# Layer norms summed tile by tile as deviations from a shift, with waits per chunk and eight stores, in a two-block model on one core

## The reference

```python
x = layer_norm(x, ln_in_g, ln_in_b)
for l in range(2):
    ...                       # three attentions from x @ w_in[l], three gates
    merged = sum(gates[:, :, n] * (branch_n @ w_branch[l, n]) for n in range(3))
    mix = merged @ w_out[l]
    x = layer_norm(2 ** 0.5 * x + mix, ln1_g[l], ln1_b[l])
    gu = x @ w_ffn_in[l]      # 1024 -> 2 x 2816
    ffn = (silu(gu[..., :2816]) * gu[..., 2816:]) @ w_ffn_out[l]
    x = layer_norm(2 ** 0.5 * x + ffn, ln2_g[l], ln2_b[l])
```

## Time and profile before

| What | us |
|---|---|
| Median of three runs (3594.59 to 3598.16) | 3596.62 |
| The profiled execution | 3600.81 |
| Its span | 3599.0 |
| PE busy in the span | 3139.0 |
| DVE, ACT, POOL busy | 1547.0, 961.6, 967.6 |

### The profile page before, as it was taken

One profiled execution on the slowest core, in us unless ns is written; L12 is line 12 of the kernel. 1 busy time (PEld: TensorE's weight loads), 2 busy tenths in 40 slices (PEclk: granted clock), 3 DMA queues, 4 the chain that ended last, 5 costly groups with the idle time before them and its releaser, 6 DMA issues.

```text
span 3599.0 us, 33188 instructions
## 1 busy us (share of the span) xinstructions
PE 3139.0 (87%) x13220; PEld 2155.6 (60%) x13220; DVE 1547.0 (43%) x2542; ACT 961.6 (27%) x1354; POOL 967.6 (27%) x353
## 2 busy tenths in 40 slices
PE   4788899878777769999899799996999999879996
PEld 3667565642222247675755578885776665568885
DVE  8895566431110131726356632223444555642223
ACT  3432223220000023425233122212333424222211
POOL 2362211310000024442211334443433212224441
PEclk9989799889999969999899899998999999989998
DMA  5214321269999942121120222221212121112220
GB/s 234 70 53 160 132 95 42 82 257 423 422 422 421 422 185 89 49 92 47 59 71 24 70 82 94 95 105 65 70 53 77 47 82 41 51 61 95 104 94 35
DMA packets 70078, 465.31 MB, mean 129 GB/s; under 512 B 8656, under 2 KB 8944, under 8 KB 17712
## 3 DMA queue, kind: packets, MB, share of 16 engines
q1 hardware_dynamic: 59184, 436.31, 31.5%
q0 software_dynamic: 5056, 16.55, 1.3%
q10 hardware_dynamic: 5696, 10.49, 0.8%
HBM read 450.71 MB, written 12.60 MB: 129 GB/s over the span
## 4 chain that ended last, share of the span: by engine, by line
PE 67%; DMA 13%; DVE 13%; ACT 2%; issue 2%; POOL 1%; SPq 0%; ACTq 0%; DVEq 0%; POOLq 0%
PE ps L424 13%; PE ps L425 13%; PE ps L426 13%; DMA mring<-w 11%; PE ps L662 3%; PE ps L645 2%; PE ps L646 2%; PE ps L647 2%; PE ps L413 2%; PE ps L2108 2%; PE ps L825 1%; DMA wring<-wfirst 1%; PE ps L677 1%; PE ps L928 1%; POOL w_lo L500 1%
## 5 line engine op out<-in xcount | busy, mean ns | idle before, releaser
L500 POOL TENSOR_TENSOR w_lo<-wring,w_hi 128x2048 fp32r<-128x2048 f32 (+1 forms) x200 | 822.6, 4120 | 1890.8 <-ACT w_hi L490 1890.7
L424 PE MATMUL ps<-x_hi,w_hi 128*128 128x512 f32 (+1 forms) x1512 | 615.2, 407 | 53.7 <-POOL w_lo L500 31.4
L426 PE MATMUL ps<-x_hi,w_lo 128*128 128x512 f32 (+1 forms) x1512 | 602.4, 398 | 0.0
L490 ACT ACTIVATE w_hi<-wring 128x2048 fp32r<-128x2048 f32 x176 | 335.6, 1910 | 515.7 <-PE ps L424 404.8
L425 PE MATMUL ps<-xf_lo,w_hi 128*128 128x512 f32 x1112 | 442.1, 398 | 0.0
L424 PEld LDWEIGHTS ps<-x_hi,w_hi 128*128 128x128 f32 (+1 forms) x1512 | 292.7, 194 | 133.3 <-issue 42.5
L426 PEld LDWEIGHTS ps<-x_hi,w_lo 128*128 128x128 f32 (+1 forms) x1512 | 292.5, 193 | 63.6
L2182 PE MATMUL ps<-mring,xT__94 128*64 128x512 f32 x512 | 245.2, 610 | 66.2 <-DMA mring<-w 60.8
L2183 PE MATMUL ps<-mring,xT__94 128*64 128x512 f32 x512 | 245.4, 610 | 0.0
L425 PEld LDWEIGHTS ps<-xf_lo,w_hi 128*128 128x128 f32 x1112 | 214.6, 193 | 43.3
L1961 DVE TENSOR_TENSOR hid<-ps,sil 64x512 f32<-64x512 f32 x32 | 21.8, 682 | 437.7 <-ACT sil L1581 437.7
(11 more groups left out here) (451 smaller groups left out, 5414.1 us busy)
## 6 DMA issues: line engine op xcount, KB each, us to landing
mring<-w SPq DMA_DIRECT2D x192, 1024.0 KB, 28.5
wring<-wlayers SPq DMA_DIRECT2D x148, 1024.0 KB, 4.7
wring<-wfirst SPq DMA_DIRECT2D x60, 1024.0 KB, 4.9
wmodS<-wmod SPq DMA_DIRECT2D x4, 2048.0 KB, 18.3
y_rows<-ysb ACTq DMA_DIRECT2D x64, 128.0 KB, 6.4
rp<-rpb POOLq DMA_DIRECT2D x16, 192.0 KB, 2.7
hT<-xT SPq DMA_DIRECT2D x1, 2048.0 KB, 18.2
xS<-xT SPq DMA_DIRECT2D x1, 2048.0 KB, 7.7
```

The source lines that it names most:

```text
L424: said(pe.matmul(bank, wh[:, 0:m], hi[:, k, :], start=(k == 0), stop=False))
L426: ins = pe.matmul(bank, wl[:, 0:m], hi[:, k, :], start=False, stop=(k == nk - 1))
L490: act.activation(w_hi[:, q % HI_SLOTS, :], wring[:, g % SLOTS, :], ACT.Copy).then_inc(hi_rdy, 1)
L500: ins = pool.tensor_tensor(w_lo[:, slot % SLOTS, o:o + n], wring[:, slot % SLOTS, o:o + n], w_hi[:, q % HI_SLOTS, o:o + n].bitcast(F32), A ...
```

## The change

**The norm** is rewritten (`norm_in_step`, with parts for PE and ACT). DVE first makes x from its two parts for all chunks (8 additions). Tiles 0 to 2 are added as they come. After tile 1 the sum of chunks 0 and 1 goes to PE (`shift_pe`, after tile 2), which gives a shift for each token, their mean. It is subtracted from chunks 0 to 2 and, before the product is there, from `DN_ALPHA * x` of chunks 3 to 7. From then on each tile takes one addition to become a deviation, one to join the sum of deviations, and one that adds the square of the tile before, made by ACT. After the last tile PE sums the deviations and the squares over partitions; the variance is the mean square less the squared mean, a small correction of the shift. The remaining mean is spread by a full-width product (bank 6), the inverse root as before (bank 7), and DVE does three instructions for each chunk: center, scale, low part.

**Other parts.**
- `weights_hi` calls stand between the squares in an order written out by `norm_in_step_act`, one for each slot start.
- In the merge ACT makes `m_hi` and DVE makes the low part of the tile before. `weights_hi` of `out2` stands after the fourth `m_hi`.
- `out2` waits for `merged_rdy` chunk by chunk in its first tile, and the first block's `out` likewise for `mix2_rdy`.
- The first two tiles of `ffn_in` (one A, one B) are made together, chunk by chunk, from weights in that order; `values` makes its first two tiles together.
- In the last norm ACT adds the bias, and SP stores each chunk by itself.
- Semaphores that nothing used are removed.

```diff
+        def norm_in_step_act(act, where, c0, nk):
+            events = [(c, 0, c) for c in range(-(c0 % CHUNKS), nk * DC, CHUNKS)]
+            events += [(nk * (max(c, 2) + 1) + (2 if c > 2 else 1), 1, c) for c in range(DC)]
+            i = cnt["ln_a"]
+            for _, kind, c in sorted(events):
+                if kind == 0:
+                    weights_hi(act, c0 + max(c, 0))
+                else:
+                    act.wait_ge(dev_rdy, DC * i + c + 1)
+                    if DC * i + c >= 2:
+                        act.wait_ge(dev_sq_in, DC * i + c - 1)
+                    act.activation(x_lo_f[where][:, 3 + c % 2, :], hT[:, c, :], ACT.Square).then_inc(dev_sq, 1)
...
+        def shift_pe(pe, where):
+            pe.wait_ge(norm_sums, 2 * cnt["ln_p"] + 1)
+            pe.matmul(ps[:, 4, :], ones, x_lo_f[where][:, 0, :], start=True, stop=True).then_inc(norm_products, 1)
+
+        def norm_in_step_pe(pe, where):
...
+            pe.wait_ge(norm_sums, 2 * i)
+            for r in range(NQB):
+                ins = pe.matmul(ps[:, 4, r:r + 1], dev[:, r * P:(r + 1) * P], ones[:, 0:1], start=True, stop=True)
+            ins.then_inc(norm_products, 1)
+            pe.wait_ge(dev_sq_in, DC * i)
+            for r in range(NQB):
+                ins = pe.matmul(ps[:, 5, r:r + 1], sq[:, r * P:(r + 1) * P], ones[:, 0:1], start=True, stop=True)
+            ins.then_inc(norm_products, 1)
+            pe.matmul(ps[:, 6, :], ones, dev, start=True, stop=True).then_inc(norm_products, 1)
+            cnt["nv_p"] += 1
+            pe.wait_ge(inv_rdy, cnt["nv_p"])
+            for r in range(NQB):
+                ins = pe.matmul(ps[:, 7, r * P:(r + 1) * P], n_inv[:, r:r + 1].broadcast_to((P, P)), ident, start=True, stop=True)
+            ins.then_inc(norm_products, 1)
...
+        def norm_in_step(dve, where, to, g, b):
...
             for c in range(DC):
+                n = mark(TT(hT[:, c, :], x_hi[:, c, :].bitcast(F32), X[:, c, :].bitcast(F32), ALU.add))
+            dve.wait_ge(dve_step, n)
+            for m in range(3):
+                STT(out=hT[:, m, :], in0=hT[:, m, :], scalar=DN_ALPHA, in1=B.take(dve), op0=ALU.mult, op1=ALU.add).then_inc(B.free, 1)
+                dve.wait_ge(B.free, B.took)
+                if m == 1:
+                    TT(shift, hT[:, 0, :], hT[:, 1, :], ALU.add).then_inc(norm_sums, 1)
+            dve.wait_ge(norm_products, 5 * i + 1)
+            step(TS(shift, ps[:, 4, :], 1.0 / (2 * P), None, ALU.mult))
+            for c in range(3):
+                TT(hT[:, c, :], hT[:, c, :], shift, ALU.subtract).then_inc(dev_rdy, 1)
+            for c in range(3, DC):
+                n = mark(STT(out=hT[:, c, :], in0=hT[:, c, :], scalar=DN_ALPHA, in1=shift, op0=ALU.mult, op1=ALU.subtract))
+            dve.wait_ge(dev_rdy, DC * i + 3)
+            step(TT(dev, hT[:, 0, :], hT[:, 1, :], ALU.add))
+            step(TT(dev, dev, hT[:, 2, :], ALU.add))
+            dve.wait_ge(dve_step, n)
+            square_in(0)
+            square_in(1)
+            for m in range(3, DC):
+                square_in(m - 1)
+                TT(hT[:, m, :], B.take(dve), hT[:, m, :], ALU.add).then_inc(dev_rdy, 1)
+                free_bank_b(dve)
+                dve.wait_ge(dev_rdy, DC * i + m + 1)
+                ins = TT(dev, dev, hT[:, m, :], ALU.add)
+                if m < DC - 1:
+                    step(ins)
+            ins.then_inc(norm_sums, 1)
+            square_in(DC - 1)
...
+            for c in range(DC):
+                if c + 1 < DC:
+                    ready.append(center(c + 1))
+                dve.wait_ge(dve_step, ready[c])
+                y = hT[:, c, :] if to is None else x_lo_f[to][:, c, :]
+                STT(out=y, in0=hT[:, c, :], scalar=g[:, c:c + 1], in1=ps[:, 7, :], op0=ALU.mult, op1=ALU.mult).then_inc(t_rdy, 1)
+                if to is not None and c >= 1:
+                    low(c - 1)
...
             def values(c0, wait=None):
-                for j in range(NQB):
-                    b = A.claim(pe)
+                for group in ((0, 1), (2,), (3,)):
+                    b = {j: A.claim(pe) for j in group}
...
-            pe.wait_ge(merged_rdy, (l + 1) * 3 * DC)
             for m in range(DC):
-                tile3(pe, B.claim(pe), base["out2"] + m * DC, m_hi, m_lo, DC).then_inc(B.full, 1)
-            mean_pe(pe)
-            norm_pe(pe, DC)
-            for m in range(FFC):
-                tile3(pe, A.claim(pe), base["ffn_in"] + 2 * m * DC, *xf, DC,
-                     wait=(lambda k: pe.wait_ge(x_rdy, 2 * DC * l + DC + k + 1)) if m == 0 else None).then_inc(A.full, 1)
+                tile3(pe, B.claim(pe), base["out2"] + m * DC, m_hi, m_lo, DC,
+                      wait=(lambda k: pe.wait_ge(merged_rdy, (3 * l + 2) * DC + k + 1)) if m == 0 else None).then_inc(B.full, 1)
+                if m == 2:
+                    shift_pe(pe, 0)
+            norm_in_step_pe(pe, 0)
+            first = A.claim(pe), B.claim(pe)
+            for k in range(DC):
+                pe.wait_ge(x_rdy, 2 * DC * l + DC + k + 1)
+                for n, b in enumerate(first):
+                    wh, wl = chunk(pe, base["ffn_in"] + 2 * k + n)
...
             for m in range(DC):
-                weights_hi(act, end1 + l * size2 + two["out2"] + m * DC)
-            squares(act, hT, DC, lambda c: act.wait_ge(centered, DC + 2 * DC * l + c + 1))
-            root(act)
+                act.wait_ge(branches_in, l * DC + m + 1)
+                act.activation(m_hi[:, m, :], uT[:, m, :], ACT.Copy, scale=0.5).then_inc(m_hi_rdy, 1)
+                if m == DC // 2 - 1:
+                    weights_hi(act, base["out2"])
+            norm_in_step_act(act, 0, base["out2"], DC)
             norm_hi(act, (V(f"ln1_b{l}"), 1))
...
+                    if m == 0:
+                        dve.wait_ge(merged_rdy, k)
+                    TT(uT[:, m, :], uT[:, m, :], g, ALU.add).then_inc(branches_in, 1)
+                    if m >= 1:
+                        merged_low(m - 1)
...
-            sp.wait_ge(x_rdy, DC + 2 * DC * LAYERS)
-            sp.dma_start(out, hT[:]).then_inc(stored, 16)
-            sp.wait_ge(stored, 16)
+            for c in range(DC):
+                sp.wait_ge(out_rdy, c + 1)
+                sp.dma_start(out[:, c, :], hT[:, c, :]).then_inc(stored, 16)
+            sp.wait_ge(stored, 16 * DC)
...
-            pe.wait_ge(mix2_rdy, DC)
             for m in range(DC):
-                tile3(pe, B.claim(pe), one["out"] + m * DC, mix_hi, mix_lo, DC).then_inc(B.full, 1)
+                tile3(pe, B.claim(pe), one["out"] + m * DC, mix_hi, mix_lo, DC,
+                      wait=(lambda k: pe.wait_ge(mix2_rdy, k + 1)) if m == 0 else None).then_inc(B.full, 1)
```

More of the change, by code:

```diff
@@ L566, in add_up @@
             dve.wait_ge(summed, cnt["sum"])
[L568 to L576, removed]
+        def shift_pe(pe, where):
+            pe.wait_ge(norm_sums, 2 * cnt["ln_p"] + 1)
+            pe.matmul(ps[:, 4, :], ones, x_lo_f[where][:, 0, :], start=True, stop=True).then_inc(norm_products, 1)
+        def norm_in_step_pe(pe, where):
+            cnt["ln_p"] += 1
+            i = cnt["ln_p"]
+            dev, sq = x_lo_f[where][:, 1, :], x_lo_f[where][:, 2, :]
+            pe.wait_ge(norm_sums, 2 * i)
[12 more added lines that the diff above has]
+            ins.then_inc(norm_products, 1)
         def mean_pe(pe):
@@ L1002, in layer_pe @@
                 tile3(pe, B.claim(pe), base["ffn_out"] + m * FFC, g_hi, g_lo, FFC,
-                     wait=(lambda k: pe.wait_ge(hid_rdy, l * FFC + k + 1)) if m == 0 else None).then_inc(B.full, 1)
-            mean_pe(pe)
-            norm_pe(pe, DC)
+                      wait=(lambda k: pe.wait_ge(hid_rdy, l * FFC + k + 1)) if m == 0 else None).then_inc(B.full, 1)
+                if m == 2:
+                    shift_pe(pe, 1)
+            norm_in_step_pe(pe, 1)
         def layer_act(act, l):
@@ L1250, in layer_dve @@
                 merge(2, m)
-            def residual(where):
-                for m in range(DC):
-                    STT(out=hT[:, m, :], in0=x_hi[:, m, :].bitcast(F32), scalar=DN_ALPHA, in1=B.take(dve), op0=ALU.mult, op1=ALU.add).then_inc(B.free, 1)
-                    dve.wait_ge(B.free, B.took)
-                    step(STT(out=hT[:, m, :], in0=x_lo[where][:, m, :].bitcast(F32), scalar=DN_ALPHA, in1=hT[:, m, :], op0=ALU.mult, op1=ALU.add))
-                    if m >= 1:
-                        add_up(dve, hT, m)
-            residual(0)
-            center(dve, hT)
-            normed_split(dve, hT, 1, V(f"ln1_g{l}"), V(f"ln1_b{l}"))
+            merged_low(DC - 1)
+            norm_in_step(dve, 0, 1, V(f"ln1_g{l}"), V(f"ln1_b{l}"))
             for m in range(FFC):
@@ L1269, in layer_dve @@
             assert a == A2 + (l + 1) * A_LAYER, (a, A2, A_LAYER)
[L1270 to L1275 removed]
+            norm_in_step(dve, 1, 0 if l < LAYERS - 1 else None, V(f"ln2_g{l}"), V(f"ln2_b{l}"))
```

(3 more changed lines are left out.)

126 lines of the change are left out of this document (80 added, 46 removed).

## The result

The changed kernel took 3538.14 us (median of four runs, 3535.15 to 3542.07) against 3595.61 us for the kernel before beside it: a ratio of 0.984, 95% interval 0.9823 to 0.9857. The forecast was 3546 with a range of 3527 to 3562; the measured time lies at the lower edge of the range of the forecast case alone, 3538 to 3556. Timed once more, on another chip, it took 3537.65 (five runs) against 3598.84, ratio 0.9834 (0.9817 to 0.9851). The profiled execution has a span of 3540.24 us, 58.8 less than before.

The account below looks back on a forecast made before the run. The prediction took TensorE, busy 87% of the span, as the bound, with gains only where it waits. Gains of 10.4 + 19.9 + 13.9 + 1.3 + 5.5 = 51.0 us gave 3546 us, range 3527 to 3562.

Parts of the forecast that it names:

- forecast case: Whole kernel: the main case, with the stall in out2 and no w_lo in the tails, 3538 to 3556 us, chance 0.54.
- LN1 and `out2`, 5.2 each: Second block's out2 and first norm: shorter tail less a stall at tile 5, 5.2 us gained per layer, 10.4 for two.
- The merge, counted as 0: Merge before out2: held low parts and a low clock at tile 4 cancel the gain; bounds 5 gained, 4 lost.
- LN2 of layer 0, 19.9: Second norm of layer 0 up to the first values tiles: tail 26.4 us in place of 47.9, 19.9 gained after deductions.
- The end, 13.9: Last norm and store: span ends 22.8 us after the last tile's first DVE instruction, before 37.6; 13.9 us gained.
- z: In each norm, the start of the first DVE instruction on the last projection tile; tail times count from it.
- The first block, 5.5: First block's out, waiting for mix2_rdy by chunk: 2.70 us idle and 2.8 us of low clock go, 5.5 gained.
- `values` of layer 0, 1.3: First two values tiles of layer 0, made together: 1.3 us gained, between 0 and 2.
- A (no stall): Rival in out2: DVE's run gets ahead of GpSimd or tile 5's bank is free in time; 3533 us, chance 0.2.
- B: Rival: a w_lo falls into the 23-instruction tail of the three inner norms, 5.1 us each; 3561 us, chance 0.17.
- C: Rival: slower by DVE alone, if the tails' 84 instructions cost over 1.27 us each; 3616 us at 1.5, chance 0.03.
- D: Rival: PE stays behind the new waits, its pair starting only when all chunks stand; 3582 us, chance 0.06.

Follow-up runs that it names:

- first moved wait: Changed kernel, but in out2's norm ACT makes the w_hi of tile 3's start only after the square of tile 3: 3529.19 us, ratio 0.9806.
- moved waits: Changed kernel, but in out2's norm ACT makes tile 3's w_hi after that tile's square and the last w_hi after the norm's eight high parts: 3515.26 us.
- moved waits and pieces together: Changed kernel with both w_hi of out2's norm made later and GpSimd's w_lo beside merge and out2 in four instructions: 3508.53 us, ratio 0.9746.
- the pieces: Changed kernel, but GpSimd makes the w_lo beside the merge and out2's first tiles in four instructions of 128x512, not one: 3519.98 us, ratio 0.9783.

## Why the prediction came out as it did

The forecast case happened: the stall in `out2` came where it was put, no `w_lo` fell into the tails, and the time was in the range. It was 8 us too slow, since three of its terms were too careful: the merge, LN2 and the end, each in part about the granted clock. That the column sums ran at full clock in both LN2 and the end was partly luck.

- **LN1 and `out2`, 5.2 each: 4.7 in layer 0 and 6.0 in layer 1 measured** (the three stretches from `out2` to the end of `ffn_out`), 10.7 for 10.4. These stretches also hold the product behind tile 2 of `ffn_out`, 0.95 in the forecast, which it took off LN2 and the end. Step by step it held: low parts of m = 0 and m = 4 held (4.64 and 4.65 us), 3.3 us idle before tile 5 (3.33), the low clock behind it, `out2` 7.0 longer (6.6, 5.5), tile 7 read 1.9 late (2.0), the pair finished 27.8 behind PE's last tile (27.9).
- **The merge, counted as 0, was the mis-sized step.** The prediction took 2.8 us for a low clock after the idle before tile 4. In layer 0 there was none (clock 1.00), and 3.7 us were gained; in layer 1 it came (0.50 at 3078), and still 2.1 were gained from the last branch's first tile to `out2` (30.4 for 32.5). The whole stretch of layer 1 doesn't show it (628.1 against 626.7), since stretches of 600 us carry clock differences of several microseconds from one execution to the next. The bounds, 5 gained to 4 lost, held both. The two stretches together gained 2.7.
- **LN2 of layer 0, 19.9: 22.5 measured**, or 21.6 with the 0.95 of the product taken off. The column sums ran at full clock, 1.05 and 1.03 in place of two times 1.87, for 1.7 us. The prediction had taken the low-clock row, though PE's idle before them was 11.89 there and is 2.05 now. But full clock was not certain: behind the same idle of 2.05 us the two groups took 1.95 to 1.99 us in seven of the twelve profiles and 2.25 to 3.35 in five. With the first moved wait, an edit that doesn't touch this norm, they ran mostly at the low clock and LN2 took 38.1 us. The hold by `w_lo` was as forecast (1.16 for 0.69). The wait for the A bank was smaller than the 0.7: PE's next matmul started 0.40 us behind the pair's last one, where 0.23 is usual.

```profile
2418.72 1.65 PE L602 MATMUL ps<-cs,uT 128*128 128x1 f32 x8 [2.05 <-DVE uT L668]
...
2420.22 1.85 PE L606 MATMUL ps<-cs,uT 128*128 128x1 f32 x8
```

- **The end, 13.9: 17.6 measured**, z + 20.1 for z + 22.8; the other 0.95 is the product, which falls before z. Column sums at full clock again 1.7 (behind an idle of 1.58; in five of the twelve profiles they took 2.15 to 3.16 us in place of 1.95); DVE's chunks 1.26 apart for 1.32, 0.5 in all; the store 2.0 us for 3.0, or 2.46 from ACT's end at 3537.78 to the end of the span, 0.5 in all. The two rows that bounded it, 192 KB in 2.7 and 1024 KB in 4.7, gave no lower end: a store of 256 KB was faster than both. The estimate from the Trainium skill's page "DMA: Bandwidth & Descriptors", section "Anatomy of one DMA — SWDGE (gpsimd) path", 2.6 for the last store by a fit for DMAs that GpSimd issues (these are SyncE's), is nearer than the 3.0, and is also above what was measured. The last store is issued at about z + 18, not z + 20.
- **The first block, 5.5: 5.6. `values` of layer 0, 1.3:** the second tile's copy followed the first matmul by 13.2 us in place of 15.2, but of these 2.0 us only 0.4 are left at the last value copy.

Of the rivals, A (no stall) didn't happen, and the moved waits show what it would have been worth: its 12 us for two layers are 10 to 15 in the stretches of `out2`, by the execution they are set against. Its cause, a DVE run that keeps GpSimd out, is excluded by the row of five in 7.50 us beside a `w_lo` of 4.86: about 0.3 lost by GpSimd, some 4 by DVE. The Trainium skill, page "SBUF — State Buffer", section "Who interferes with whom", has the issue order decide who blocks; the trace agrees in the sense that GpSimd enters between two DVE instructions and then holds the next for its whole length. The run with moved waits and pieces together shows that this costs the changed kernel 27 us by the stretches and 29 by the medians. B fell by the absence of any held instruction between the spread and the last low part; C by a pace of 0.64 us an instruction; D by PE's first pair matmul at 14 us behind the last tile, not behind all chunks.

## What to carry to other kernels

When sums over a tensor are moved into the production of its tiles, the instructions that used to follow now compete with everything that runs beside the tiles; look for the engine whose instructions hold the summing one's (here GpSimd's `w_lo`, 4.6 us each), move its work by where it is requested, or cut it into pieces, before counting the gain. A tail that waits on a chunked producer gains when two consumers share each chunk (14 us here), and to a wait of PE belongs the low clock that may follow it, which can be bounded but not counted on.

## What the runs showed of the hardware that was not expected

- Idle PE of 2.66 us was followed by no fall of the granted clock (1983.25), by one that came 1.5 us later and lasted some 3 (1997.12), and in layer 1 by the low clock at once (3091.39). The gap of 3.3 us at tile 5 of `out2` was followed by 3.4 us at half clock eleven times in eighteen, by 5.4 to 5.7 six times and by none once (the pieces, layer 1). A matmul takes 0.427 us at half clock in place of 0.227, so 5.7 us of it cost some 2.7, and gaps of this size are a risk with a price of 0 to 3 us, not a fixed cost.
- In the merge the clock fell behind one of two idles of PE or behind neither, never behind both. In 12 of 18 merges (nine changed kernels with whole `w_lo` and the wait per chunk, two layers each) PE had run at half clock for 3.3 to 3.4 us behind its idle of 2.13 us before the branch's first tile; in none of them did the clock fall at tile 4. In the other six it fell there in five, for 3.9 to 4.0 us. Why is not shown.
- GpSimd's subtraction in four pieces costs it 1.8 us more and hands DVE back 3.3 us for each instruction of two SBUF operands that falls beside it.
- One 2 MB store of SBUF to memory took 6.3 us and eight of 256 KB 2.0 each, spread over the time in which they are made.
